# Another order for the head and for the last third of the mixing stage of a hybrid decoder layer

## What is computed

```python
mod = silu(c) @ w_ada + b_ada                       # 6 x 1024 values per sequence: shifts, scales, gates
h = rmsnorm(x, norm1_g) * (1 + sc1) + sh1
xr, gr, q, k, v, o, ig, fg, u = split(h @ w_in)     # 384 each for the first six, 4, 4, 256
y_a = rglru(causal_dwconv(xr)) * gelu(gr)           # recurrence over positions
y_b = sigmoid(o) * rmsnorm(mlstm(q, k, v, ig, fg))  # 4 heads of 96, 8 chunks of 128 positions
y_c = pool_mix(u)                                   # windows 2, 4, 8, 16: (mean - u) @ pool_w * pool_scale
x = x + gt1 * (concat(y_a, y_b, y_c) @ w_out)
h2 = rmsnorm(x, norm2_g) * (1 + sc2) + sh2
x = x + gt2 * (square(relu(h2 @ w_ff1)) @ w_ff2)
y = rmsnorm(x, final_g)                             # and the new states
```

## Time and profile before

| what | us |
|---|---|
| median of 3 runs | 1169.37 |
| lowest and highest of them | 1166.39, 1173.94 |
| the profiled execution's own time | 1164.52 |
| its span, first to last instruction | 1162.7 |
| mixing stage in it | 0 to about 371 |

### The profile page before, as it was taken

One profiled execution on the slowest core, in us unless ns is written; L12 is line 12 of the kernel. 1 busy time (PEld: TensorE's weight loads), 2 busy tenths in 40 slices (PEclk: granted clock), 3 DMA queues, 4 the chain that ended last, 5 costly groups with the idle time before them and its releaser, 6 DMA issues.

```text
span 1162.7 us, 19579 instructions
## 1 busy us (share of the span) xinstructions
PE 1116.7 (96%) x7205; PEld 1070.1 (92%) x7205; DVE 798.7 (69%) x1318; ACT 468.2 (40%) x766; POOL 343.4 (30%) x273
## 2 busy tenths in 40 slices
PE   5899999899889999899999999999999999999997
PEld 2688888799879999899999999999999999999996
DVE  5662255678875433777679778778788788788546
ACT  5552446454555343641332332432432433433431
POOL 1240101200535366762032122121231231231342
PEclk9999999999989999999999999999999999999998
DMA  9814423857334722110111202102202102111104
GB/s 342 306 58 144 113 91 128 233 157 230 120 110 134 246 73 73 37 57 36 40 34 58 70 19 74 56 16 72 72 18 72 54 22 86 36 54 55 37 1 146
DMA packets 76037, 109.85 MB, mean 94 GB/s; under 512 B 6434, under 2 KB 58950, under 8 KB 75590
## 3 DMA queue, kind: packets, MB, share of 16 engines
q1 hardware_dynamic: 58598, 84.88, 22.2%
q10 hardware_dynamic: 17376, 24.12, 6.7%
HBM read 96.81 MB, written 12.18 MB: 94 GB/s over the span
## 4 chain that ended last, share of the span: by engine, by line
PE 77%; DVE 13%; DMA 4%; ACT 3%; issue 1%; POOL 1%; SPq 1%; ACTq 0%; POOLq 0%; DVEq 0%
PE D L2459 6%; PE D L2643 6%; PE D L2645 6%; PE D L2644 6%; PE D L2461 5%; PE D L2460 5%; PE X L2645 5%; PE X L2643 5%; PE X L2644 5%; PE X L2715 5%; PE X L2717 5%; PE X L2716 5%; PE D L2715 2%; PE D L2717 2%; PE D L2716 2%; DMA SPARE<-in_WADA 2%
## 5 line engine op out<-in xcount | busy, mean ns | idle before, releaser
L2459 PE MATMUL D<-H_hi,W_hi 128*128 128x344 f32 x472 | 158.7, 336 | 4.7 <-POOL H_lo L1120 3.9
L2461 PE MATMUL D<-H_hi,W_lo 128*128 128x344 f32 x472 | 152.1, 322 | 0.0
L2460 PE MATMUL D<-H_lo,W_hi 128*128 128x344 f32 x472 | 152.0, 322 | 0.0
L1120 POOL TENSOR_TENSOR Y_lo<-FU,Y_hi 128x344 fp32r<-128x344 f32 (+3 forms) x84 | 100.2, 1196 | 153.7 <-ACT Y_hi L1556 87.5
L1115 POOL TENSOR_TENSOR W_lo<-RAWW,W_hi 128x1024 fp32r<-128x1024 f32 x25 | 61.4, 2458 | 179.9 <-ACT W_hi L1269 179.6
L2459 PEld LDWEIGHTS D<-H_hi,W_hi 128*128 128x128 f32 x472 | 90.2, 191 | 15.3 <-issue 9.5
L1120 POOL TENSOR_TENSOR Y_lo<-EY,Y_hi 128x344 fp32r<-128x344 f32 (+1 forms) x24 | 38.4, 1599 | 216.3 <-ACT Y_hi L1556 144.5
L2460 PEld LDWEIGHTS D<-H_lo,W_hi 128*128 128x128 f32 x472 | 90.1, 191 | 0.6 <-issue 0.2
L2461 PEld LDWEIGHTS D<-H_hi,W_lo 128*128 128x128 f32 x472 | 89.8, 190 | 0.0
L2261 DVE SCALAR_TENSOR_TENSOR X<-X,MOD 128x344 f32<-128x344 f32 (+1 forms) x138 | 75.7, 567 | 9.2 <-PE X L2717 9.1
L2715 PE MATMUL X<-Y_hi,W_hi 128*128 128x344 f32 x252 | 80.7, 320 | 0.0
(11 more groups left out here) (420 smaller groups left out, 3426.6 us busy)
## 6 DMA issues: line engine op xcount, KB each, us to landing
RAWW<-in_W SPq DMA_DIRECT2D x76, 512.0 KB, 3.6
RAWW<-in_WADA ACTq DMA_DIRECT2D x28, 512.0 KB, 3.7
RAWW<-in_W ACTq DMA_DIRECT2D x18, 512.0 KB, 3.9
RAWW<-in_WADA SPq DMA_DIRECT2D x12, 512.0 KB, 10.9
X0T<-in_x SPq DMA_DIRECT2D x3, 1376.0 KB, 12.0
out_y<-OUTN SPq DMA_DIRECT2D x24, 172.0 KB
SPARE<-in_WADA SPq DMA_DIRECT2D x8, 512.0 KB, 11.2
X<-in_x SPq DMA_DIRECT2D x8, 344.0 KB, 4.5
```

What stands on the lines that cost most here:

```text
L1120: nc.gpsimd.tensor_tensor(lo_v, fu_v, hi_v.bitcast(F32), ALU.subtract).then_inc(lo_ready, 1)
L2459: T.matmul(out, w_h, hi[:, kt, a:b], start=(kt == 0), stop=False)
L2460: T.matmul(out, w_h, lo[:, kt, a:b], start=False, stop=False)
L2461: one = T.matmul(out, w_l, hi[:, kt, a:b], start=False, stop=(kt == KT - 1))
```

## The change

Six edits, of which four are only places in MIX_ORDER:
- The loads of c, cols and the identity are issued by ACT, ahead of its first instruction, instead of SP.
- WV_lo of K pairs 1 and 3 is made by POOL, that of 0 and 2 still by DVE. V:0 waits for each pair in turn.
- V:1 and V:2 are cut: VK:1:0:5 and VK:2:0:6 do their first K tiles ahead of NS:1 and NS:2, V:1 and V:2 the rest behind.
- ADA:8:1 to ADA:8:3 stand behind V:1 instead of in and behind the chunks 1 and 2.
- ADM:14 stands behind D:13:2 instead of D:14:0. D:15:0 stands ahead of POOL:0:0 and what follows it, D:15:1 ahead of POOL:1:0 and the rest of the second pooling group; POOL:1:2 is now ahead of S:7.
- W:17 stands in D:15:2's line instead of D:16:1's.

```diff
--- before.py
+++ after.py
@@ -103,7 +103,7 @@
 WV:2 DK:0:0:7:8
 WV:3 DK:1:0:7:8
 D:0:0 SQ:1:0
-D:1:0 SQ:1:1 V:0 NS:1 ADA:8:0 N:1:0 N:1:1 V:1 N:1:2 N:1:3 DK:0:1:0:1
+D:1:0 SQ:1:1 V:0 VK:1:0:5 NS:1 ADA:8:0 N:1:0 N:1:1 V:1 ADA:8:1 ADA:8:2 N:1:2 ADA:8:3 N:1:3 DK:0:1:0:1
 DK:1:1:0:1
 N:1:4 DK:0:1:1:2
 DK:1:1:1:2
@@ -113,17 +113,17 @@
 DK:1:1:3:4
 N:1:7 DK:0:1:4:5
 DK:1:1:4:5
-R:12 ADA:8:1 DK:0:1:5:6
+R:12 DK:0:1:5:6
 SQ:2:0 DK:1:1:5:6
 DK:0:1:6:7
 DK:1:1:6:7
 SQ:2:1 DK:0:1:7:8
 DK:1:1:7:8
 D:0:1
-D:1:1 V:2 NS:2 N:2:8 N:2:0 R:13 N:2:1 N:2:2 V:3 N:2:3 N:2:4 N:2:5 N:2:6 V:4 N:2:7 DK:0:2:0:8
+D:1:1 VK:2:0:6 NS:2 V:2 N:2:8 N:2:0 R:13 N:2:1 N:2:2 V:3 N:2:3 N:2:4 N:2:5 N:2:6 V:4 N:2:7 DK:0:2:0:8
 W:2 V:5
 D:0:2 R:14 DK:1:2:0:8
-ADA:8:2 ADA:8:3 R:15 V:6 V:7 W:3 V:8 R:17 ADT:8
+R:15 V:6 V:7 W:3 V:8 R:17 ADT:8
 D:1:2 ADM:8 ADA:9:0 G1 ADA:9:1
 D:2:0 R:16
 D:2:1 R:18 G2
@@ -160,16 +160,15 @@
 D:12:2 R:48 U:4 HN:4 W:14 YD:0 R:50 HM:4 LD:6
 D:13:0 Y:1 CN:4 ADA:14:2 EX:5 YD:1 R:49
 D:13:1 S:5 ADA:14:3 POOLV:0 YS POOLS:0 POOLD:0 SX:5 W:15 YSD AB:5 NU:5 HN:5 HM:5
-D:13:2 ADT:14 R:51 U:5 CN:5
-D:14:0 Y:2 ADM:14 EX:6 YD:2
+D:13:2 ADT:14 R:51 U:5 CN:5 ADM:14
+D:14:0 Y:2 EX:6 YD:2
 D:14:1 ADA:15:0 S:6 SX:6 R:53 AB:6 ADA:15:1 Y:3 POOLV:1
-D:14:2 POOL:0:0 POOLS:1 NU:6 YD:3 R:52 POOLY:0:0 POOL:0:1 POOLY:0:1 HN:6 LD:7 POOL:0:2 POOLD:1 POOLY:0:2
-    HM:6
-D:15:0 U:6 Y:4 POOL:1:0 R:54 CN:6 POOLY:1:0 ADA:15:2 EX:7 POOL:1:1 W:16 R:56 YD:4
-D:15:1 POOLY:1:1 S:7 SX:7 POOL:1:2 POOLY:1:2 ADA:15:3 R:55
-D:15:2 Y:5 YD:5 AB:7 NU:7 ADT:15 HN:7
+D:14:2 NU:6
+D:15:0 POOL:0:0 POOLS:1 YD:3 R:52 POOLY:0:0 POOL:0:1 POOLY:0:1 HN:6 LD:7 POOL:0:2 POOLD:1 POOLY:0:2 HM:6 U:6 Y:4 R:54 CN:6 EX:7
+D:15:1 POOL:1:0 POOLY:1:0 ADA:15:2 POOL:1:1 W:16 R:56 YD:4 POOLY:1:1 POOL:1:2 S:7 SX:7 POOLY:1:2 ADA:15:3 R:55
+D:15:2 Y:5 YD:5 AB:7 NU:7 ADT:15 W:17 HN:7
 D:16:0 R:57 HM:7 Y:6 U:7 YD:6 CN:7 ADM:15
-D:16:1 Y:7 W:17 YD:7
+D:16:1 Y:7 YD:7
 D:16:2
 """
 
@@ -515,7 +514,7 @@
         ld_w = [sem(f"ld_w{u}") for u in range(N_EARLY_W)]
         ld_xres = [sem(f"ld_xres{m}") for m in range(KT)]
         ones_ready, sig_c, c_ready = sem("ones_ready"), sem("sig_c"), sem("c_ready")
-        wv_hi, wv_lo = sem("wv_hi"), sem("wv_lo")
+        wv_hi, wv_lo, wv_lo_pool = sem("wv_hi"), sem("wv_lo"), sem("wv_lo_pool")
         v_ready, v8_ready, v8_stored = sem("v_ready"), sem("v8_ready"), sem("v8_stored")
         v_stored = [sem(f"v_stored{b}") for b in range(2)]
         st_stored = [sem(f"st_stored{b}") for b in range(2)]
@@ -831,9 +830,6 @@
             def load_o(c):
                 sp.dma_start(OT[:], o_d.rearrange("(j p) t -> p j t", p=P)[:, :, c * LC:(c + 1) * LC]).then_inc(ld_o, 16)
 
-            sp.dma_start(CTX[:, 0:CW], I["c"].rearrange("p k b -> p (k b)")).then_inc(ld_c, 16)
-            sp.dma_start(COLS[:], I["cols"]).then_inc(ld_cols, 16)
-            sp.dma_start(IDN[:], I["ident"]).then_inc(ld_idn, 16)
             load_x(0)
             for n, key in enumerate(sp_raws):
                 if key in SPARE_PIECES:
@@ -1145,6 +1141,11 @@
                         w_lo(s[1], raw_slot(s[1]), s[1] % 2)
                 elif k == "N":
                     lo(full_at[s], *views(s))
+                elif k == "WV" and s[1] % 2:
+                    k0 = 2 * s[1]
+                    pool.wait_ge(wv_hi, s[1] + 1)
+                    nc.gpsimd.tensor_tensor(WV_lo[:, k0:k0 + 2, :], WV_raw[:, k0:k0 + 2, :], WV_hi[:, k0:k0 + 2, :].bitcast(F32),
+                                            ALU.subtract).then_inc(wv_lo_pool, 1)
                 elif k == "D":
                     if s in full_at:
                         lo(full_at[s], *views(s))
@@ -1292,6 +1293,9 @@
                 nc.scalar.activation(SS[:, c * CH:(c + 1) * CH], bank(norm)[:, 0:CH], ACT.Sqrt, bias=EPT[:], scale=1.0 / D
                                      ).then_inc(root_ready, 1)
 
+            act.dma_start(CTX[:, 0:CW], I["c"].rearrange("p k b -> p (k b)")).then_inc(ld_c, 16)
+            act.dma_start(COLS[:], I["cols"]).then_inc(ld_cols, 16)
+            act.dma_start(IDN[:], I["ident"]).then_inc(ld_idn, 16)
             act.wait_ge(ld_c, 16)
             nc.scalar.activation(CTS[:], CTX[:, 0:CW], ACT.Sigmoid).then_inc(sig_c, 1)
 
@@ -1817,7 +1821,7 @@
                     u = s[1]
                     dve.wait_ge(w_hi_ready, u + 1)
                     V.tensor_tensor(W_lo[:, u, :], WR[u][:], W_hi[:, u, :].bitcast(F32), ALU.subtract).then_inc(w_lo_ready, 1)
-                elif k == "WV":
+                elif k == "WV" and s[1] % 2 == 0:
                     k0 = 2 * s[1]
                     dve.wait_ge(wv_hi, s[1] + 1)
                     V.tensor_tensor(WV_lo[:, k0:k0 + 2, :], WV_raw[:, k0:k0 + 2, :], WV_hi[:, k0:k0 + 2, :].bitcast(F32), ALU.subtract).then_inc(wv_lo, 1)
@@ -2462,6 +2466,7 @@
                 if k1 == KT:
                     one.then_inc(d_full[bank], 1)
 
+            v_split = {}
             pe.wait_ge(c_ready, 1)
             pe.wait_ge(sel_ready, 2)
             pe.wait_ge(ones_ready, 7)
@@ -2473,20 +2478,28 @@
                     ada(s[1], s[2])
                 elif k == "ADT":
                     ada_turn(s)
-                elif k == "V":
+                elif k in ("V", "VK"):
 
                     t = s[1]
+                    key = ("V", t)
                     a = t * LC
                     m = min(LC, TOK - a)
-                    pe.wait_ge(wv_lo, 4)
-                    pe.wait_ge(lo_ready, norm_done((a + m - 1) // CH))
-                    ps = take(s)
-                    for kt in range(KT):
+                    k0, k1 = s[2:] if k == "VK" else (v_split.get(t, 0), KT)
+                    if k0 == 0:
+                        pe.wait_ge(lo_ready, norm_done((a + m - 1) // CH))
+                        take(key)
+                    if k == "VK":
+                        v_split[t] = k1
+                    ps = bank(key)
+                    for kt in range(k0, k1):
+                        if t == 0 and kt % 2 == 0:
+                            pe.wait_ge((wv_lo, wv_lo_pool)[kt // 2 % 2], kt // 4 + 1)
                         h, l = H_hi[:, kt, a:a + m], H_lo[:, kt, a:a + m]
                         T.matmul(ps[0:m, 0:VCOLS], h, WV_hi[:, kt, :], start=(kt == 0), stop=False)
                         T.matmul(ps[0:m, 0:VCOLS], h, WV_lo[:, kt, :], start=False, stop=False)
                         one = T.matmul(ps[0:m, 0:VCOLS], l, WV_hi[:, kt, :], start=False, stop=(kt == KT - 1))
-                    done(one, s)
+                    if k1 == KT:
+                        done(one, key)
                 elif k == "D":
                     _, u, c = s
                     if u >= 2:
```

## The result

The changed kernel takes 1172.04 us (median; 1169.42 to 1178.02), the kernel before on the same chip 1167.26 us. The ratio is 1.0047, with a 95% interval from 1.0035 to 1.0060: about 5.5 us slower. The forecast was a gain of 2.0 us. The sign is wrong, and rival C, at +2.4 us, had the direction and the place, but less than half of the size. (The forecast's 1167.4 us was counted from a median of three runs, 1169.4. From the median of twenty it would be 1165.3.)

What follows compares the result with a forecast made beforehand. TensorE, busy 96% of the span, bounds the kernel, so only its waits and half clock can yield time. Head -2.3 and last third +0.3 give -2.0 us: 1162.5 for the profiled execution, 1167.4 as median, range 1161.5 to 1172.0.

Steps and rivals of the forecast that it cites:

- rival C: Last third: half clock returns behind POOL:1:2, on S:7, ADA:15:3 and D:15:2; +2.4 us in all, 1171.8; chance 0.20.
- Early small loads, -1.3: Head: small loads on ScalarE's queue let x and each load behind it go out 1.37 us sooner; -1.3 us.
- The delayed c is covered: Head: c's later load costs nothing, as PE's first matmul waits to 10.15 for a w_ada piece; uncovered, 1.4 us.
- squares and sums start only some 0.6 sooner: Head: bound of -0.6 us on the loads' gain, as ScalarE issues the three before its first table load.
- Rival B: Head: ScalarE's and VectorE's norm chain, not landings, sets 23 to 41 us; loads win 0.3, sum -1.0, 1168.4; chance 0.17.
- V by K pairs and half of WV_lo on GpSimd, 0: Head: V:0 ends sooner, but sums of squares and NS:1 slip beside GpSimd; 0 us, bounds -1.4 and +2.0.
- rival A: Head and W:17: VectorE and GpSimd do not hold each other up; -5.9 us in all, 1163.5; chance 0.18.
- ADA pieces, -1.0: Head: ADA:8:1 to 8:3 go into PE's wait for N:1; -1.0 us, or 0 if they delay DK:0:1.
- The last third without W:17, -0.8: Last third of mixing: D:15:0 forward gains 0.6 us of D:15:1's 6 us lead, with ADM:14 -0.8 us.
- EX:7's operands at about 342.7: Last third: when ScalarE's exponential could start, in the chain that lets POOL:1:2 run at 347.4.
- D:15:2 starts at 349.9: Last third: behind POOL:1:2, S:7 and ADA:15:3, D:15:2 starts at 349.9 instead of 350.5, a gain of 0.6 us.
- W:17, +1.1: End of last third: GpSimd's W_lo(17) stretches HN:7 on VectorE, Y:7 slips 2.1 us; +1.1 us, bounds -1.4 and +1.2.

Runs made afterwards that it cites:

- e1: Changed kernel with the last third of MIX_ORDER (D:13:2 to D:16:2) as before, so the head's edits alone; ratio 0.9997 to the kernel before.
- e4: Changed kernel with W:17 put back late, behind Y:7; ratio 1.0023 to the kernel before.
- e5: Changed kernel with S:7 and SX:7 ahead of POOL:1:2; ratio 1.0028 to the kernel before.
- e6: Changed kernel with POOL:1:2 and POOLY:1:2 moved behind Y:6; ratio 1.0029 to the kernel before.
- e12: Kernel before with one edit, c, cols and ident issued from ScalarE's queue; ratio 1.0009 to the kernel before.
- e2: Kernel before with only the last third of MIX_ORDER (D:13:2 to D:16:2) as changed; ratio 1.0053 to the kernel before.
- e3: Changed kernel with the three small loads back ahead of x on SP's queue; ratio 1.0038 to the kernel before.
- e8: Kernel before's head with the changed last third, POOL:1:2 moved behind Y:6 and the early W_lo(17) made on VectorE; ratio 0.9998 to the kernel before.
- e14: Changed kernel, loads on SP, all WV_lo and W_lo(17) on VectorE, EX:7 behind D:15:1's gelu, POOLY:0:0, YD:6, HM:7 earlier; 1161.0 us, ratio 0.9943 to kernel before.
- e11: Changed kernel with all four WV_lo on VectorE, V still by K pairs; ratio 1.0033 to the kernel before.
- e7: Kernel before with W:17 early, W_hi(17) ahead of HN:7's root and W_lo(17) on VectorE instead of GpSimd; ratio 0.9992 to the kernel before.

## Why the prediction was wrong, step by step

**Early small loads, -1.3: wrong sign, as far as single executions show it.** "The delayed c is covered" held, since PE still waited for the piece. What failed is the bound "squares and sums start only some 0.6 sooner": I counted the issue (0.38 for one) but gave the landings the time that they had alone. They started 1.4 later; measured +1.2 (e1, e4, e5, e6, e12 against e2, e3, e8, e14). Rival B had the right chain and still thought it a gain.

**V by K pairs and half of WV_lo on GpSimd, 0: right, and for the reason given.** NS:1 was to slip 1.55 us and DK:0:1 1.6; counted from MOD both slipped 1.6. PE was to end the chunk at 64.6: in e3 it is 64.8 on the same count. Only the half clock behind DK:0:1's wait, 1.0 us, was not in the sum. Another half clock was not either: with the late rise the head of the kernel before runs at half clock from about 8 us behind MOD and takes 70.2 us (e2, e8, e12), the changed one's 69.0 as before (e1, e4, e5, e6). So with the late rise these edits and the ADA pieces together win 1.2 us, with the early rise nothing, which may be how e1 came out at -0.4 in spite of the loads. "The two engines hold each other up" decided it against rival A, and e11 shows that the whole loss was GpSimd's half.

**ADA pieces, -1.0: right** as far as the runs can split it. e3's stretch, 68.0, is 1.0 under the 69.0 of e7, which has the head of the kernel before, and both ran at full clock there; e3 has it with NS:1 1.6 later. The pieces were never run alone.

**The last third without W:17, -0.8: this step failed.** From Y:3 to Y:5, where W:17 has no part, the changed kernel took 34.6 us against 30.5: +4.0 (e4, which has all of it but W:17, +3.5). ADM:14 did what was forecast, since PE's wait of 1.47 us became 0.71. Two other terms were off. "EX:7's operands at about 342.7": on the forecast's clock (Y:3 stood 1.4 us later in the changed kernel) the exponential began at 344.3, since DVE's two steps on EX (0.69 each) and the wait for NM stood before it. And "D:15:2 starts at 349.9" priced S:7 and ADA:15:3 at full clock; they and D:15:2 ran at half, as rival C said: D:15:2 began at 352.9, and Y:5 came 4.0 later than before. C had 0.20, because I took a wait of 3.1 us to lie between one that had dropped the clock and one that had not; it became 3.7. Beneath the sizes is a step that I had not taken. I priced the chain behind EX:7 and never asked what a matmul is worth whose eviction does not come along. D:15:1 moved forward by 5.0 us on PE (344.0 to 340.45 - 1.42), its gelu by 3.1 (349.4 to 347.70 - 1.42), and four things behind the gelu, not one, keep PE waiting: X1 by POOLY:1:0, X3 by YD:4, and through them S:7 and D:15:2.

**W:17, +1.1: right, in mechanism and nearly in size.** Y:7 was to slip 2.1 us, and from Y:5 to Y:7 it is 13.25 us against 11.15. OUT:0's wait of 1.52 goes and OUT:1's weights bind instead, 0.73 us in the changed kernel: behind Y:5 +1.2 in all, and 1.6 and 1.7 in e3 and e11, where OUT:1 waits 1.03 and 1.17.

**Sum.** Forecast -2.3 and +0.3. Measured, last third +5.3 (4.0 and 1.2, rounded). The head is -0.4 by e1's medians, with an interval from -2.5 to +1.6, and +1.2 by the stretches of the early kind (loads +1.2, the rest 0). Together +4.9 or +6.5, both within the interval of the ratio, 4.1 to 7.0 us.

## What to carry to other kernels

When a matmul is moved forward, move its eviction with it: look at what stands ahead of it on the evicting engine, since an exponential that waits there, with its table loads, holds every bank behind. A short chain of small instructions on one engine is no place to hide a long one of another that it shares operands' memory with; give the work to the engine that waits anyway. And a load is not early because it is issued early: what goes out beside it decides when it lands.
